# Convolution of a Mamba-2 branch: the centre tap moves from VectorE to ScalarE

## What is computed

```python
def mamba2_bidir(z, xbc, dt_raw, conv_w, conv_b, dt_bias, A_log, D_skip, norm_g):
    b, l, ch = xbc.shape
    pad = SSM_CONV // 2
    xbc = lax.conv_general_dilated(xbc, conv_w[:, None, :], window_strides=(1,),
                                   padding=[(pad, pad)], dimension_numbers=('NWC', 'WIO', 'NWC'),
                                   feature_group_count=ch) + conv_b
    xbc = jax.nn.silu(xbc)
    xs, Bm, Cm = split_cols(xbc, (SSM_INNER, SSM_BC_COLS, SSM_BC_COLS))
```

## Time and profile before

| | |
|---|---|
| runs | 1639.74, 1646.62, 1644.38 us; median 1644.38 us |
| profiled execution | 1639.83 us, its span 1638.1 us |
| TensorE matmul, weight load | busy 1527.2 us and 1454.0 us |
| VectorE, ScalarE, GpSimd | busy 1063.9, 788.4 and 410.4 us |
| mean granted TensorE clock | 0.976 of full speed |
| DMA | 238.39 MB, 146 GB/s |
| copy to `cin`, line 828 | 12 times, 226.4 to 1115.7 us |

### The profile page before, as it was taken

The page is one execution under the profiler, slowest core; times in us unless marked ns, Lnnn a source line. Parts: engine busy times, 40 slices in busy tenths (PEclk is TensorE's granted clock), DMA queues, the critical chain, the costliest instruction groups (busy, mean ns, idle before and its releaser), DMA issues.

```text
span 1638.1 us, 30327 instructions
## 1 busy us (share of the span) xinstructions
PE 1527.2 (93%) x11327; PEld 1454.0 (89%) x11327; DVE 1063.9 (65%) x1352; ACT 788.4 (48%) x1077; POOL 410.4 (25%) x227
## 2 busy tenths in 40 slices
PE   4999887989989999999999998888998899999997
PEld 4899787868978999999999987786898899999997
DVE  5544569998887646554443555999888874565543
ACT  4444557754333445444444545676433344454453
POOL 3310000022212144454434000001221213354442
PEclk9999999999989999999999999999999999999998
DMA  5544333443333455656545434344433245555552
GB/s 175 186 143 135 117 104 105 140 141 105 119 113 113 154 172 162 198 174 218 175 156 178 138 117 129 103 120 128 139 117 103 90 155 181 168 171 189 187 201 101
DMA packets 149140, 238.39 MB, mean 146 GB/s; under 512 B 11665, under 2 KB 57611, under 8 KB 149003
## 3 DMA queue, kind: packets, MB, share of 16 engines
q1 hardware_dynamic: 147339, 235.11, 45.6%
q10 hardware_dynamic: 1664, 1.48, 0.3%
HBM read 235.50 MB, written 1.05 MB: 144 GB/s over the span
## 4 chain that ended last, share of the span: by engine, by line
PE 56%; DVE 20%; DVEq 10%; ACT 7%; issue 5%; ACTq 2%; DMA 1%
PE PS L498 51%; DVE wL L1150 5%; PE S L498 4%; DVE regA L1374 3%; ACT wH L806 3%; DVEq L1371 2%; DVE actL L1394 2%; DVEq L1416 2%; DVEq L1397 1%; DVE scr L1414 1%; DVE actH L1394 1%; DVE small L1332 1%; DVEq L1331 1%; ACT scr L923 1%; ACTq L974 1%
## 5 line engine op out<-in xcount | busy, mean ns | idle before, releaser
L1150 DVE TENSOR_TENSOR wL<-w_raw,wH 128x1024 fp32r<-128x1024 f32 (+1 forms) x330 | 472.9, 1440 | 368.7 <-ACT wH L806 353.7
L806 ACT CAST wH<-w_raw 128x1024 fp32r<-128x1024 f32 (+1 forms) x443 | 453.4, 1041 | 250.2 <-PE PS L498 219.5
L498 PE MATMUL PS<-hH,wH 128*128 128x256 f32 x1856 | 544.8, 294 | 4.1 <-DVE wL L1150 4.1
L498 PE MATMUL PS<-hL,wH 128*128 128x256 f32 x1856 | 534.2, 288 | 0.0
L498 PE MATMUL PS<-hH,wL 128*128 128x256 f32 x1856 | 534.0, 288 | 0.0
L1066 POOL TENSOR_TENSOR wL<-w_raw,wH 128x1024 fp32r<-128x1024 f32 (+1 forms) x113 | 297.2, 2634 | 438.2 <-ACT wH L806 438.2
L498 PEld LDWEIGHTS PS<-hH,wH 128*128 128x128 f32 x1856 | 365.8, 197 | 11.3 <-issue 6.4
L498 PEld LDWEIGHTS PS<-hL,wH 128*128 128x128 f32 x1856 | 365.7, 197 | 1.9 <-issue 1.4
L498 PEld LDWEIGHTS PS<-hH,wL 128*128 128x128 f32 x1856 | 365.3, 197 | 0.0
L498 PE MATMUL PS<-actH,wH 128*128 128x256 f32 x1120 | 324.7, 290 | 8.3 <-DVE wL L1150 2.9
L498 PE MATMUL PS<-actH,wL 128*128 128x256 f32 x1120 | 319.2, 285 | 0.0
(11 more groups left out here) (231 smaller groups left out, 1603.4 us busy)
## 6 DMA issues: line engine op xcount, KB each, us to landing
w_raw<-in_w_in_dram SPq DMA_DIRECT2D x192, 512.0 KB
w_raw<-in_w_ffn_in_dram SPq DMA_DIRECT2D x176, 256.0 KB
w_raw<-in_w_branch_dram SPq DMA_DIRECT2D x64, 512.0 KB
w_raw<-in_w_ffn_out_dram SPq DMA_DIRECT2D x44, 512.0 KB
w_raw<-in_w_mem_kv_dram SPq DMA_DIRECT2D x35, 512.0 KB
w_raw<-in_w_out_dram SPq DMA_DIRECT2D x16, 512.0 KB
regA<-in_mem_dram SPq DMA_DIRECT2D x6, 512.0 KB, 5.1
scr<-in_x_dram ACTq DMA_DIRECT2D x1, 1024.0 KB, 11.1
```

The source lines that it names most:

```text
L498: return nc.tensor.matmul(o, l, r, start=first, stop=last, skip_group_check=True)
L806: nc.scalar.copy(wH[:, slot].rearrange("p k c -> p (k c)")[:, q], raw[:, slot].rearrange("p k c -> p (k c)")[:, q]).then_inc(h_done[slot], 1)
L1150: v.tensor_tensor(wL[:, slot].rearrange("p k c -> p (k c)")[:, q], raw[:, slot].rearrange("p k c -> p (k c)")[:, q], wH[:, slot].rearrange ...
```

## The change

ScalarE now also computes the centre tap. Before its copy to `cin` it reads the four tiles in PSUM and writes `w2 * x + bias` to `cacc` with four ACTIVATE (function Identity, scale and bias each a column of 128 values). VectorE no longer starts `cacc` with tap 0 and the bias; all of its taps, 0, 1, 3 and 4, accumulate, and one drain a step goes. The wait that keeps `cacc` until its last content is transposed (`xs_turned`) moves from VectorE's conv step to ScalarE's evacuation. Below line 828 the new kernel's line numbers are 7 higher, and from the conv step on 2 higher.

```diff
--- before.py
+++ after.py
@@ -825,6 +825,13 @@
                         act.wait_ge(da_copied, HEADS * lay + 1)
                     else:
                         act.wait_ge(conv_done, 6 * lay + b)
+                    if b >= 2:
+                        act.wait_ge(xs_turned, 8 * lay + 2 * b - 2)
+                    for j in range(4):
+                        t = 4 * b + j
+                        nc.scalar.activation(cacc[b % 2][:, j, :], src[:, T * j:T * (j + 1)], ACT.Identity,
+                                             bias=p_cb[:, t:t + 1],
+                                             scale=p_cw[:, CONV_T * 2 + t:CONV_T * 2 + t + 1])
                     nc.scalar.copy(cin[:, :, 2:2 + T], v3(src[:, :], 4)).then_inc(psum_free[pair], 1)
                 elif kind == "z":
                     wait_full(act, lay, g)
@@ -1360,15 +1367,10 @@
                     b, g = i // 2, GI["xbc", i // 2]
                     if i % 2 == 0:
                         dve.wait_ge(psum_free[g % 2], used_after(lay, g))
-                        if b >= 2:
-                            dve.wait_ge(xs_turned, 8 * lay + 2 * b - 2)
                     js = range(2 * (i % 2), 2 * (i % 2) + 2)
-                    for j in js:
-                        t = 4 * b + j
-                        v.tensor_scalar(cacc[b % 2][:, j, :], cin[:, j, 0:T], p_cw[:, t:t + 1], p_cb[:, t:t + 1],
-                                        ALU.mult, ALU.add)
-                    for k in range(1, CONV):
-                        dve.drain()
+                    for k in (0, 1, 3, 4):
+                        if k > 0:
+                            dve.drain()
                         for j in js:
                             q = CONV_T * k + 4 * b + j
                             v.scalar_tensor_tensor(cacc[b % 2][:, j, :], cin[:, j, k:k + T], p_cw[:, q:q + 1],
```

## The result

The changed kernel takes 1646.71 us (median of 20 runs, 1643.52 to 1648.80), the kernel before 1642.33 us (20 runs, 1637.59 to 1646.62). The ratio is 1.0027 with a 95% interval of 1.0018 to 1.0036: 4.4 us slower, 3.0 to 5.9. That is under the 0.5% set as the line of "no change", and it is where the forecast had it, on the slow side. So taking 18.7 us of busy time off VectorE bought nothing.

The account below looks back on a forecast made before the run. A VectorE-ScalarE loop was taken to bound the convolution stage: +1.88 us ScalarE minus 1.62 us VectorE, 0.26 us over 12 blocks, +3.1 us. The three-run median plus this gave 1647.5, put at 1646.5 us; range 1637.8 to 1654.9.

Parts of the forecast that it names:

- What bounds the stage: Convolution stage of the xbc blocks: a loop of VectorE and ScalarE sets the 18.54 us period, not TensorE.
- the 0.17 us wait: VectorE's wait at its own half of the split for ScalarE's second split; forecast to grow to about 2 us.
- the four waits of the earlier trace: VectorE's waits between 245 and 322 us in the kernel before, all ascribed to ScalarE's second split, 1.0 us in total.
- What VectorE loses: In the two conv steps, the tensor_scalar pair goes: 0.82 and 0.80 us, 1.62 us a block, all on the loop.
- What ScalarE gains: Four ACTIVATE from PSUM before the copy to cin, 0.47 us each start to start, 1.88 us a block.
- Where it lands: Between ScalarE's first split and the copy; everything behind comes 1.88 us later, so a mid-stage block changes by +0.26 us.
- the silu's wait: ScalarE's silu waiting for VectorE's second conv step; forecast to fall from 1.91 to 0.3 us.
- The sum: Over both layers' convolution stages: 12 blocks times 0.26 us, +3.1 us for the kernel.
- six equal blocks: Each layer's six xbc blocks, including blocks 0 and 5, were counted with the same +0.26 us.
- The total: Whole kernel: median of three runs plus 3.1 us gives 1647.5 us, with the new median put at 1646.5 us.

Follow-up runs that it names:

- the constant-scale run: The changed kernel with the four ACTIVATE's scale an immediate 0.5 instead of the weight column, bias still a column: 1639.49 us, 0.9991 of before.
- the first experiments: The first four follow-up experiments, run on one chip beside executions of the kernel before, whose median there was 1642.21 us.
- the small-instruction run: The kernel before with one 128-column ACTIVATE a block added ahead of the copy, writing where nothing reads: 1643.79 us, 1.0011 of before.

## Why the prediction was right

- **What bounds the stage.** Right. The place to look was not VectorE's 92% but the 0.17 us wait, which showed that ScalarE had no slack at that point. (Of the four waits of the earlier trace rows three are for this split; the fourth, 0.19 us at 305.03, is for the one ahead of it.) Doing the four twice gave 21.9 us for an expected 21.7.
- **What VectorE loses.** 1.62 us a block forecast. The kernel without the four shows 18.54 - 16.86 = 1.68 us in mid-stage and 18.3 us in the stages, against 19.4. The forecast left out the two 0.4 us idle times in a layer that every kernel with the shorter VectorE code shows; with one of them, block 3 of the changed kernel is 0.46 us longer than before where its neighbour, block 2, is 0.15 us longer.
- **What ScalarE gains.** 0.47 us each was forecast, 0.452 us measured; 1.81 us a block in place of 1.88. The step was worked from one column at 128x256 and the added column at 128x512, and the constant-scale run confirms its structure: 0.472 us with one column, 0.562 us with two, 0.11 us of overlap in both the forecast and the rows. The Trainium skill's page "ScalarE: Activation LUTs", under "What ACT_TABLE_LOAD costs", gives 0.49 us as an estimate by its formula; the measurement decides for 0.45 us here, with the cost of a pointer operand (93 ns on the page, 0.09 us here) confirmed.
- **Where it lands.** The wait for the split was to go to about 2 us in each block (2.00, 2.00, 2.01 and 1.94 us in four of them; in block 1 VectorE waits 1.3 us for ScalarE at another instruction, line 1165), the silu's wait to 0.3 us (0.28 and 0.23), the period to 18.8 us (18.69), VectorE's busy time down by 18 us (18.7), ScalarE's up by 23 us (21.9).
- **The sum.** +3.1 us forecast, +2.2 us in the stages, +4.4 us (3.0 to 5.9) in the medians. The mechanism held and the size in the stages was too large by 0.9 us, nearly all of it the 0.07 us a block by which the four ACTIVATE were priced too high (12 x 0.07 = 0.8 us). That six equal blocks came out so well is partly luck: VectorE's new idle time in block 3 and the one that ScalarE loses in block 4, neither of them in the forecast, cancel (0.27 us above 0.19 and 0.28 us below it).
- **The total.** That the median of 1646.71 us is 0.2 us from the forecast 1646.5 is luck. The forecast stood on the median of three executions, 1644.38, which is 2.1 us above that of twenty; 1.0 us was taken off without a stage to take it from; and the change came out 1.3 us larger than the sum.
- **What is not explained.** The other 2.2 us of the medians lie outside the stages. There the kernel before alone moved by 6.8 us between two profiles. But the interval of the change, 3.0 to 5.9 us, does not hold 2.2 us, so chance in the choice of executions is not a likely answer. The 20 executions of the changed kernel had a mean clock of 0.970 to 0.975, the 19 of before beside the first experiments 0.973 to 0.978. That is a hint and no more: part of it is clock in the stages (0.97 before, 0.95 changed in the first two profiles), where it costs nothing. Whether the change lowers the clock outside them is open, and the small-instruction run was too blunt to tell.

## What to carry over

Moving work off the busiest engine paid here only where the receiving engine had slack at the place where the work landed. Its idle share doesn't say so (ScalarE was 27% idle in each period); the wait of the one for the other, at that spot in the order, does. When a move cancels itself like this, try the place before giving up the move: with the evacuation one position later the kernel was 18 us faster than before instead of 4 us slower, and 14.6 us of that are the tap's.

## What I had not expected

The time between the two stages, and with it most of the spread of the totals, moves with TensorE's granted clock. Two windows of 30 us at about the same place of the program, 570 us after the last silu of the first layer, in the first profile of before (upper line) and of the changed kernel (lower line):

```profile
904.90:934.90 30.00, 30.00 (x232) 29.26 (x231) 17.60 (x34) 16.98 (x27) 0.00 (x0) 1.00 0.48 148
```

```profile
903.80:933.80 30.00, 30.00 (x202) 29.37 (x202) 15.28 (x32) 14.74 (x23) 0.00 (x0) 0.86 0.42 123
```

TensorE counts as fully busy in both, but in the second the clock is at its lower level (1.2 in place of 2.4 GHz) for part of the window, 0.86 on average, and 202 matmuls are done in place of 232. At 232 in 30 us, 30 matmuls are 3.9 us. The kernel before by itself has both a shorter and a longer stretch: its two profiles took 686.75 us with a mean clock of 0.99 and 693.52 us with 0.98 there. The second is from another chip than the experiments, but one chip is enough for the spread: the 19 executions of before beside the first experiments took 1639.28 to 1648.14 us, the seven up to 1641.5 us at a mean clock of 0.977 or 0.978 and the five above 1645 us at 0.973 to 0.975. What lowers the clock in one execution and not in the next no run here shows. The stages, meanwhile, repeat to 0.04 us between profiles. In a kernel like this a change of 2 us can be read from the stage it touches in one profile to a tenth of a microsecond, and less well from twenty total times.
